# Loading order and first steps of a two-block fp32 kernel: token tiles in 2, 2, 2, 4, 6 columns on two queues, a first granule in two halves, a zero copy on ScalarE, three zero products on TensorE

## The reference

```python
h = rms_norm(x, ln_pre_g[layer])                        # x: 256 x 2048
proj = jnp.einsum('bsd,de->bse', h, w_in[layer])        # the first products of the program
rnn_x, rnn_gate, q, k, v, attn_gate, g_rnn, g_attn = split_columns(proj)
```

## Time and profile before

| | before |
|---|---|
| median of 3 runs | 2542.69 us (2540.52 to 2544.24) |
| time of the profiled execution | 2541.07 us |
| its span in the profile | 2539.3 us |
| TensorE busy | 2508.7 us, 99% |
| VectorE busy | 1946.3 us, 77% |
| ScalarE busy | 1273.2 us, 50% |
| first product of weights starts at | 10.16 us |

### The profile page before, as it was taken

One profiled execution on the slowest core, in us unless ns is written; L12 is line 12 of the kernel. 1 busy time (PEld: TensorE's weight loads), 2 busy tenths in 40 slices (PEclk: granted clock), 3 DMA queues, 4 the chain that ended last, 5 costly groups with the idle time before them and its releaser, 6 DMA issues.

```text
span 2539.3 us, 30959 instructions
## 1 busy us (share of the span) xinstructions
PE 2508.7 (99%) x11974; PEld 2047.7 (81%) x11974; DVE 1946.3 (77%) x2685; ACT 1273.2 (50%) x1754; POOL 98.8 (4%) x143
## 2 busy tenths in 40 slices
PE   8999999999999999999999999999999999999998
PEld 6778777888888888888888888778888888888887
DVE  6776776887776777566978768998985887998866
ACT  6544544545553444455456644436565454455654
POOL 0000000000000000000200000200000000200000
PEclk9999999999999999999999999999999999999999
DMA  9887798566556666676555568654446879544454
GB/s 351 307 308 261 252 317 279 196 215 216 194 182 239 234 241 242 234 258 230 182 164 165 171 244 290 236 166 150 157 145 245 292 257 348 198 147 153 149 190 174
DMA packets 350594, 570.15 MB, mean 225 GB/s; under 512 B 18224, under 2 KB 202800, under 8 KB 346608
## 3 DMA queue, kind: packets, MB, share of 16 engines
q1 hardware_dynamic: 343216, 532.84, 61.2%
q0 software_dynamic: 6512, 34.59, 3.8%
q10 hardware_dynamic: 720, 0.75, 0.1%
HBM read 559.69 MB, written 8.41 MB: 224 GB/s over the span
## 4 chain that ended last, share of the span: by engine, by line
PE 91%; DVE 3%; DMA 3%; ACT 1%; issue 1%; POOL 0%; SPq 0%; DVEq 0%; ACTq 0%
PE acc L587 27%; PE acc L589 27%; PE acc L588 27%; PE aux L1236 2%; PE aux L1261 1%; DVE w_lo L575 1%; DVE rows_u L2142 1%; PE aux L1018 1%; PE aux L1385 1%; DMA xr_s<-x_mid 1%; DMA xr_s<-c_mid 1%; PE aux L1246 1%; DMA rows_in<-in_w_mod 1%; PE aux L880 1%; ACT w_hi L567 0%
## 5 line engine op out<-in xcount | busy, mean ns | idle before, releaser
L575 DVE TENSOR_TENSOR w_lo<-raw,w_hi 128x1024 fp32r<-128x1024 f32 x808 | 990.6, 1229 | 446.5 <-ACT w_hi L567 444.5
L567 ACT ACTIVATE w_hi<-raw 128x1024 fp32r<-128x1024 f32 x808 | 847.1, 1059 | 870.2 <-PE acc L589 806.2
L587 PE MATMUL acc<-w_hi,h_hi 128*128 128x512 f32 x2240 | 893.1, 399 | 15.6 <-DVE w_lo L575 15.6
L589 PE MATMUL acc<-w_hi,h_lo 128*128 128x512 f32 x2240 | 875.4, 391 | 0.0
L588 PE MATMUL acc<-w_lo,h_hi 128*128 128x512 f32 x2240 | 874.3, 390 | 0.0
L587 PEld LDWEIGHTS acc<-w_hi,h_hi 128*128 128x128 f32 x2240 | 422.1, 188 | 120.9 <-issue 26.6
L589 PEld LDWEIGHTS acc<-w_hi,h_lo 128*128 128x128 f32 x2240 | 421.6, 188 | 90.1
L588 PEld LDWEIGHTS acc<-w_lo,h_hi 128*128 128x128 f32 x2240 | 422.5, 189 | 83.7
L587 PE MATMUL acc<-w_hi,u_hi 128*128 128x512 f32 x800 | 318.8, 398 | 1.5 <-DVE w_lo L575 1.4
L589 PE MATMUL acc<-w_hi,u_lo 128*128 128x512 f32 x800 | 312.1, 390 | 0.0
L588 PE MATMUL acc<-w_lo,u_hi 128*128 128x512 f32 x800 | 311.8, 390 | 0.0
(11 more groups left out here) (356 smaller groups left out, 2016.8 us busy)
## 6 DMA issues: line engine op xcount, KB each, us to landing
raw<-in_w_in SPq DMA_DIRECT2D x631, 512.0 KB, 4.7
raw<-in_w_mod SPq DMA_DIRECT2D x112, 512.0 KB, 6.2
raw<-in_w_out SPq DMA_DIRECT2D x96, 512.0 KB, 4.7
rows_in<-in_w_mod SPq DMA_DIRECT2D x80, 512.0 KB, 6.7
raw<-in_w_rnn_out SPq DMA_DIRECT2D x32, 512.0 KB, 4.6
raw<-in_w_o SPq DMA_DIRECT2D x32, 512.0 KB, 5.7
raw<-in_w_attn_out SPq DMA_DIRECT2D x16, 512.0 KB, 5.7
xr_s<-x_mid POOLq DMA_DIRECT2D x4, 1024.0 KB, 13.7
```

Source lines behind the costliest of these rows:

```text
L567: act.activation(w_hi[:, n % NSPLIT], raw[:, slot, (n % 2) * SK:(n % 2) * SK + SK], ACT.Copy).then_inc(hi_ready, 1)
L575: dve.tensor_tensor(w_lo[:, n % NSPLIT], raw[:, slot, (n % 2) * SK:(n % 2) * SK + SK], w_hi[:, n % NSPLIT].bitcast(F32), ALU.subtract).the ...
L587: pe.matmul(acc[pair][m][:, :], a_hi[:, k0 + k, tok], w_hi[:, s, k], start=b, stop=False)
L589: last = pe.matmul(acc[pair][m][:, :], a_lo[:, k0 + k, tok], w_hi[:, s, k], start=False, stop=e)
```

## The change

- **Turned tokens.** Five transfers of 2, 2, 2, 4 and 6 column tiles. The first is issued by ScalarE on its own queue, ahead of its constants; the others by SyncE, between the parts of pairs 0, 1 and 3.
- **First granule by k tile.** The two k tiles of granule 0 come in transfers of 256 KB with a semaphore each; ScalarE copies, VectorE subtracts and TensorE multiplies them one by one. The count of `lo_ready` is one higher from then on. Pair 1 comes in parts too, with granule 2 signalled by itself.
- **Zero copy.** ScalarE copies one column of zeros before its first wait on the tokens, which puts the table load there.
- **Zero products.** TensorE does three instead of one.
- **Constants.** `cols_b`, `ident` and `modbias` are issued by ScalarE after `hi` of granules 3, 4 and 5, and share one semaphore: who needs one of them waits for all three.
- **Straight tokens and tables.** `xr` is issued behind pair 5 and pair 6 instead of pair 4 and pair 5. Both transfers, `rope1` and `mask1` share one semaphore, `x_in`: who needs one of them waits for all four (64).

```diff
+TOKEN_ENDS = (0, 2, 4, 6, 10, 16)
+WARM = 3
...
-            if n == 0 and fresh:
-                act.wait_ge(first_raw, 16)
-            elif n % 2 == 0 or fresh and n == 1:
+            if n == 2 and fresh:
+                act.wait_ge(early_raw[2], 16)
+            elif n % 2 == 0 and (n or not fresh) or fresh and n in (1, 3):
...
+            if n == 0 and fresh:
+
+                for k in range(SK):
+                    act.wait_ge(early_raw[k], 16)
+                    act.activation(w_hi[:, 0, k], raw[:, slot, k], ACT.Copy).then_inc(hi_ready, 1)
+                return
...
+            if q + n == 0:
+
+                for k in range(SK):
+                    dve.wait_ge(hi_ready, k + 1)
+                    dve.tensor_tensor(w_lo[:, 0, k], raw[:, slot, k], w_hi[:, 0, k].bitcast(F32), ALU.subtract).then_inc(lo_ready, 1)
+                return
...
+                if q + n == 0:
+                    pe.wait_ge(lo_ready, k + 1)
...
-                sp.dma_start(xr[:, m], t["x"][0][m * P:(m + 1) * P, :]).then_inc((x_in, x_in1)[m], 16)
+                sp.dma_start(xr[:, m], t["x"][0][m * P:(m + 1) * P, :]).then_inc(x_in, 16)
...
-                if place in (NLOAD, NLOAD + 1):
-                    tokens(place - NLOAD)
+                if place in (NLOAD + 1, NLOAD + 2):
+                    tokens(place - NLOAD - 1)
                 if kind == "pair" and i == 5:
-                    sp.dma_start(rope1[:, :, :, :], t["rope_table"]).then_inc(table_in, 16)
-                    sp.dma_start(mask1[:, :, :], t["dilated_masks"]).then_inc(table_in, 16)
+                    sp.dma_start(rope1[:, :, :, :], t["rope_table"]).then_inc(x_in, 16)
+                    sp.dma_start(mask1[:, :, :], t["dilated_masks"]).then_inc(x_in, 16)
...
-            pe.matmul(X[3][:, :], modchunk[:, 0:P], modchunk[:, :], start=True, stop=True)
+            for _ in range(WARM):
+                pe.matmul(X[3][:, :], modchunk[:, 0:P], modchunk[:, :], start=True, stop=True)
...
+            act.dma_start(xT[:, 0:TOKEN_ENDS[1], :], t["x_columns"][:, 0:TOKEN_ENDS[1], :]).then_inc(xT_in[0], 16)
             act.dma_start(cols_a[:, :], t["columns"][:, 0:P]).then_inc(cols_a_in, 16)
...
+            act.wait_ge(mod_zero, 1)
+            act.activation(small[:, 41:42], modchunk[:, 0:1], ACT.Copy)
...
                 hi(act, Q1, b, b < NSPLIT)
+                if b == 3:
+                    act.dma_start(cols_b[:, 0:COLS_B], t["columns"][:, P:P + COLS_B]).then_inc(cols_b_in, 16)
+                elif b == 4:
+                    act.dma_start(ident[:, :], t["identity"]).then_inc(cols_b_in, 16)
+                elif b == 5:
+                    act.dma_start(modbias[:, :], t["columns"][:, P + COLS_B:P + COLS_B + 2 * LAYERS * KT]).then_inc(cols_b_in, 16)
...
-                        act.wait_ge((x_in, x_in1)[m], 16)
+                        act.wait_ge(x_in, 64)
                         act.activation(xr[:, m], xr[:, m], ACT.Square, accum_out=small[:, m:m + 1]).then_inc(ss_ready, 1)
...
-                dve.wait_ge(table_in, 32)
+                dve.wait_ge(x_in, 64)
```

More of the change, by code:

```diff
@@ L403, in build_program @@
         hi_ready, lo_ready, split_used = (sem(n) for n in ("hi_ready", "lo_ready", "split_used"))
-        const_in, x_in, xT_in = sem("const_in"), sem("x_in"), [sem(f"xT_in{i}") for i in range(4)]
-        cols_a_in, cols_b_in, first_raw = sem("cols_a_in"), sem("cols_b_in"), sem("first_raw")
+        x_in, xT_in = sem("x_in"), [sem(f"xT_in{i}") for i in range(5)]
+        cols_a_in, cols_b_in, early_raw = sem("cols_a_in"), sem("cols_b_in"), [sem(f"early_raw{i}") for i in range(3)]
         sp_ready, spn_ready, token_scale = sem("sp_ready"), sem("spn_ready"), sem("token_scale")
@@ L445, in build_program @@
         cv_sig, smod_r = sem("cv_sig"), sem("smod_r")
-        table_in, x_in1 = sem("table_in"), sem("x_in1")
         weighted, final_rstd, results = sem("weighted"), sem("final_rstd"), [sem(f"result{i}") for i in range(3)]
@@ L487, in load @@
                 if kind == "pair":
-                    sp.wait_ge(lo_ready, 2 * i + 2)
+                    sp.wait_ge(lo_ready, 2 * i + 3)
                 elif kind == "part":
@@ L572, in lo @@
             slot = slot_of(("pair", (q + n) // 2))
-            dve.wait_ge(hi_ready, q + (n + 1))
+            if q + n == 0:
[3 more added lines that the diff above has]
+                return
+            dve.wait_ge(hi_ready, q + (n + 2))
             dve.tensor_tensor(w_lo[:, n % NSPLIT], raw[:, slot, (n % 2) * SK:(n % 2) * SK + SK],
@@ L578, in products @@
         def products(pe, q, n, pair, k0, a_hi, a_lo, start, stop, tiles=range(NT)):
-            pe.wait_ge(lo_ready, q + (n + 1))
+            if q + n:
+                pe.wait_ge(lo_ready, q + (n + 2))
             s = n % NSPLIT
             for k in range(SK):
+                if q + n == 0:
+                    pe.wait_ge(lo_ready, k + 1)
                 for m in tiles:
@@ L621, in turned_tokens @@
             def turned_tokens(g):
-                k = slice(LK * g, LK * (g + 1))
+                k = slice(TOKEN_ENDS[g], TOKEN_ENDS[g + 1])
                 sp.dma_start(xT[:, k, :], t["x_columns"][:, k, :]).then_inc(xT_in[g], 16)
             def tokens(m):
-                sp.dma_start(xr[:, m], t["x"][0][m * P:(m + 1) * P, :]).then_inc((x_in, x_in1)[m], 16)
+                sp.dma_start(xr[:, m], t["x"][0][m * P:(m + 1) * P, :]).then_inc(x_in, 16)
             def gate_weights(it):
@@ L686, in _ @@
                 place = PLACE[item]
[L687 to L691, removed]
+                if place == 3:
+                    turned_tokens(4)
+                if place < 2:
+                    src = ktiles(w1, place, ds(0, CH))
+                    if place == 0:
+                        for k in range(SK):
+                            sp.dma_start(raw[:, 0, k, :], src[:, k, :]).then_inc(early_raw[k], 16)
+                    else:
+                        sp.dma_start(raw[:, 1, 0:SK, :], src[:, 0:SK, :]).then_inc(early_raw[2], 16)
+                    turned_tokens(1 + 2 * place)
                     for k in (2, 3):
-                        sp.dma_start(raw[:, 0, k, :], src[:, k, :]).then_inc(raw_ready[0], 16)
+                        sp.dma_start(raw[:, place, k, :], src[:, k, :]).then_inc(raw_ready[place], 16)
+                    if place == 0:
+                        turned_tokens(2)
                 elif kind == "pair":
@@ L949, in t_rnn @@
                 if first:
-                    pe.wait_ge(const_in, 16)
+                    pe.wait_ge(cols_b_in, 48)
                 else:
@@ L1103, in branch_granule @@
                 if n == 8:
-                    pe.wait_ge(table_in, 32)
+                    pe.wait_ge(x_in, 64)
                     pe.wait_ge(ev1_act, CH1 * IT1)
@@ L1458, in norm_sides @@
                     norm_high(s + 1, n - batches - 2, aff, dst)
+            act.dma_start(xT[:, 0:TOKEN_ENDS[1], :], t["x_columns"][:, 0:TOKEN_ENDS[1], :]).then_inc(xT_in[0], 16)
             act.dma_start(cols_a[:, :], t["columns"][:, 0:P]).then_inc(cols_a_in, 16)
-            act.dma_start(cols_b[:, 0:COLS_B], t["columns"][:, P:P + COLS_B]).then_inc(cols_b_in, 16)
-            act.dma_start(ident[:, :], t["identity"]).then_inc(const_in, 16)
-            act.dma_start(modbias[:, :], t["columns"][:, P + COLS_B:P + COLS_B + 2 * LAYERS * KT]).then_inc(cols_b_in, 16)
+            act.wait_ge(mod_zero, 1)
+            act.activation(small[:, 41:42], modchunk[:, 0:1], ACT.Copy)
             act.wait_ge(cols_a_in, 16)
             for b in range(8):
-                if b % 2 == 0:
-                    act.wait_ge(xT_in[b // 2], 16)
+                if 2 * b in TOKEN_ENDS:
+                    act.wait_ge(xT_in[TOKEN_ENDS.index(2 * b)], 16)
                 for k in (2 * b, 2 * b + 1):
@@ L1547, in iteration @@
                     if first and n == 8:
-                        act.wait_ge(cols_b_in, 32)
+                        act.wait_ge(cols_b_in, 48)
                         act.activation(scs[:, :], cols_b[:, CV:CV + 2 * KT], ACT.Sigmoid).then_inc(cv_sig, 1)
@@ L2200, in iteration @@
                     if first and n == 8:
-                        dve.wait_ge(cols_b_in, 32)
+                        dve.wait_ge(cols_b_in, 48)
                         softplus_start()
```

## The result

| | before | changed |
|---|---|---|
| median | 2542.69 us (9 runs, 2540.52 to 2549.40) | 2549.57 us (9 runs, 2546.19 to 2552.72) |
| ratio to before | | 1.0022, 95% interval 1.0013 to 1.0030 |
| profiled execution | 2541.07 us, span 2539.3 us | 2551.47 us, span 2549.7 us |
| TensorE busy | 2508.7 us, 99% | 2517.2 us, 99% |

The account below looks back on a forecast made before the run. TensorE is 99% busy, but ScalarE and VectorE lead from 33 to 95 us. Sums of squares +3.9, less 0.3 for the emptier queue, start not counted: +3.6 us, 2546.3 us from 2542.69, range 2540 to 2549.5.

Parts of the forecast that it names:

- The chain: From 33 us to 95 us ScalarE and VectorE lead, not TensorE; what hangs on them and is late stays late.
- wait before granule 11: TensorE, ahead from the start, waits 1.2 to 2.4 us for granule 11's w_lo, and its gain is gone.
- The term that decides: ScalarE's first sum of squares waits for the last straight tokens, landing at 37.3 instead of starting at 33.38: 3.9 us late.
- second queue: Issuing on ScalarE's queue adds no bandwidth; if it did, the last straight tokens would land 0.7 us earlier.
- The deduction: Loads of w_mod after the late sums land up to 0.9 us sooner in an emptier queue; 0.3 was taken off.
- The start: First product at 8.9 instead of 10.16 us; TensorE 1.2 to 2.4 us ahead by granule 1, not counted in the sum.
- All of it or nothing: Three zero products keep TensorE's clock high for the first products, saving 1.2 us wholly or not at all.
- Rival B: Clock falls in TensorE's new waits, and slow products after the tile at 59 us outlast the chain: +5.3, 2548.0; chance 0.22.
- Rival A: The straight tokens land in time and the start's gain stays: -1.2 to -2.4, say 2540.5; chance 0.15.
- C: The delay is worn off by slack in VectorE's row before 95 us: about 2542.5; chance 0.08.
- within 0.2%: Whole time within 0.2% (5 us) of before, on the slow side; chance 0.76.
- slower by over 0.2%: Whole time more than 0.2% above before, most of it from the clock falling in new waits; chance 0.2.

Follow-up runs that it names:

- x_early_apart: Changed kernel with straight tokens behind pair 4 and pair 5 again and each sum of squares waiting for its own half alone; ratio to before 0.9993.
- x_later_shared: Changed kernel with the second half of the straight tokens one pair further back, behind pair 7; ratio to before 1.0030.
- second profile: Changed kernel run and profiled once more, with nothing altered; ratio to before 1.0014, +3.6 us.
- before_late_shared: Kernel before with straight tokens behind pair 5 and pair 6 and one shared wait for both halves and both tables, old start kept; ratio to before 1.0012.
- x_late_apart: Changed kernel with its order of loads, but each sum of squares waiting for its own half alone; ratio to before 1.0008.
- x_early_shared: Changed kernel with straight tokens behind pair 4 and pair 5 again, shared wait for both halves and both tables kept; ratio to before 1.0007.
- x_early_apart_warm1: The kernel x_early_apart with one zero product instead of three; ratio to before 0.9997.

## Why the prediction was right, and where it was short

**The chain.** That the time from 33 to 95 us is led by ScalarE and VectorE and not by TensorE is the step on which all rested, and it is shown: the delay at granule 12 follows the start of the sums of squares to a tenth in six profiles of five kernels (4.48 and 4.5, 4.10 and 4.1, 7.73 and 7.7, 4.17 and 4.2, 1.36 and 1.4, and 1.78 and 1.8 by the second sum), and at granule 28 it is there within 0.5, save the 1.3 of one transfer in one profile. From x_early_apart to x_later_shared the ratios rise with it from 0.9993 to 1.0030. And TensorE's own lead does not count: its wait before granule 11 is 3.57, 1.21 and 6.49 us in three profiles with the new start, and the delay is that of the sums of squares each time.

**The term that decides.** The landing was put at 37.3, where the last half of pair 6 had landed, and the delay at 3.9. Measured were 37.86 and 37.48, delays of 4.5 and 4.1. The mechanism, the same bytes in another order in a full queue, held: the DMA engines have no gap there (share 0.97 or more in every stretch of 2 us from 8 to 42 us), and one more pair, 1 MB, ahead of the load in `x_later_shared` moves it by 3.3 to 3.6 us more. The term was 0.2 to 0.6 too small. No bandwidth of a second queue shows: had it added bandwidth, the landing would have been 0.7 us sooner, at 36.6, and it was later than 37.3.

**The deduction.** I took 0.3 off for an emptier queue. In the second profile, 4.1 shrank to 3.7 on the way to granule 28, in before_late_shared 4.2 to 4.0. But in x_late_apart and x_later_shared nothing came off (1.8 and 1.8, 7.7 and 7.8), and in the first profile and x_early_shared the delay grew, by 1.3 and 0.5. So the deduction is not borne out as a term; where something came off, it was 0.2 to 0.4.

**The start.** First product foretold at 8.9, measured at 8.38: the first transfers landed sooner (cols_a let h_hi go at 5.74; I had taken 6.3, from 5.8 to 6.8). In the second profile it let h_hi go at 6.09, and the first product stands at 8.74. The zero products took 5.49 and 5.30 us instead of 6.2. "All of it or nothing" for the clock came out both ways: up from the first product on in one profile, down from 9.8 to 13 us in the other. So the wait before granule 11 was 3.57 us in the one and 1.21 in the other, where I had 1.2 to 2.4, and nothing came of the difference, as forecast.

**The rivals.** Rival B has the number nearest to the first set of runs (2548.0 against 2548.3), but not by its mechanism. It wanted a wait of 2.4 to 3 us for the tile at 59 us and slow products behind it. In the first profile TensorE has no such wait; in the second it waits 1.01 us, until 59.02; the clock is 1.00 from 50 to 64 us in both. The clock did fall at granule 11, at 42 us, in the first profile, and was back at 48; those slow products were hidden by the chain, as the prediction said. Rival A (tokens in time) and C (worn off) did not come about. What A would have been worth is tested by x_early_apart: at granule 28 it is 0.4 us late, and of A's 1.2 to 2.4 us nothing shows there; its time, 1.8 us faster, does not tell A's price from none.

**What is short.** The prediction was +3.6 us; the two sets of runs say +5.6 (3.3 to 7.6) and +3.6 (1.3 to 5.8). I gave 0.76 to "within 0.2%", where the second set lies (0.14%), and 0.2 to "slower by over 0.2%", where the first lies (0.22%, with 0.13% as its lower end). The mechanism of the sum held. Its sizes fell short in two places: the term of the sums of squares, by 0.2 to 0.6 us, and all that lies beyond 95 us, for which the sum has no term. In the first profile the delay is 5.8 us at granule 28 and 10.4 at the end; in the second it is 3.7 and 4.5, after a stretch at 5.8 to 6.0. The largest single step between is at 781 us, where TensorE waits 2.5 us for VectorE in every profile. In that of before, the clock stayed up, and the products behind the wait stand 0.23 to 0.24 us apart:

```profile
775.78 1.17 PE L918 MATMUL aux<-ident,s_sb 128*128 128x128 f32 x9 [2.47 <-DVE og L2058]
...
777.02 0.40 PE L588 MATMUL acc<-w_lo,u_hi 128*128 128x512 f32 x1
777.26 0.39 PE L589 MATMUL acc<-w_hi,u_lo 128*128 128x512 f32 x1
```

In the first profile of the change it fell (the last row is a window, with the granted clock behind the count), the products stand 0.43 us apart, and the granules behind them are another 1.6 us later:

```profile
781.48 1.68 PE L941 MATMUL aux<-ident,s_sb 128*128 128x128 f32 x9 [2.48 <-DVE og L2088]
...
783.81 0.63 PE L605 MATMUL acc<-w_hi,u_lo 128*128 128x512 f32 x1
784.24 0.63 PE L603 MATMUL acc<-w_hi,u_hi 128*128 128x512 f32 x1
```

```profile
780.00:784.00 4.00, 2.52 (x12) 0.75 0.00 0
```

The clock fell there in 7 of 12 profiles: in both of the changed kernel and in five with its start, but not in before_late_shared nor in three others with that start. Whether the change makes it likelier, by moving everything ahead of it, can't be told from so few; it is not settled whether anything is left of the difference once such steps are evened out.

**Where the start's gain goes.** Even with the straight tokens in time it is not seen in the profiles by granule 28, nor clearly in the times: the ratios of the four kernels with tokens in time are 0.9993 to 0.9998, each with 1 inside its interval, and a gain of up to some 4 us is not excluded. In the kernels with the new start TensorE begins 1.4 to 1.8 us earlier and granule 2 is split 1.6 to 2.5 us earlier, but from 10 to 48 us the DMA queue is full (share 0.97 to 1.19 in every stretch of 2 us, before and with the change), and granule 6 is split no earlier than before (0 to 0.8 us later). With the tokens in time the chain is within 0.7 us of where it was at granule 28, and not ahead at the last tile of w_mod. That the queue holds it is what ScalarE's wait on pair 5 shows at granule 10; further on (granules 12 to 28) it is argued from TensorE's and VectorE's waits on w_mod, and was not taken away by itself.

## What to carry to other kernels

A semaphore shared by several loads turns a wait for the first into a wait for the last, and a load moved back in a full queue lands later by all the bytes that now stand ahead of it: here 4.1 to 4.5 us, more than twice the 1.4 to 1.8 us by which the first product came earlier. Before the start of a kernel is tuned, follow the chain of waits beyond it: here a lead of the busiest engine was worth nothing that the runs can show, since other engines and a full queue lead a few granules on. When semaphores are short, let loads share one that are issued next to each other and needed at the same time.

## What was not expected of the hardware

- The three zero products took between 4.3 and 5.5 us in eight profiles with the same start, and what was left as a wait before the first product went with the clock there: after waits of 1.5 to 1.8 us (four profiles) it stayed up, after 2.1 to 2.9 us (four, the second one of the change among them: 0.94 from 8 to 10 us, 0.50 from 10 to 12) it fell. Which of the two, the wait or the moment at which the zero products ended, decides is not shown, as they come together.
- A wait of TensorE of 2.5 us at the same place left the clock up in five profiles and was followed by a fall in seven (0.75 over the 4 us in the first profile of the change); the length of the wait alone does not decide. The longer waits, 3.57 us up to 42 us and 6.49 us in x_later_shared up to 45 us, were both followed by windows at 0.50.
- Windows of the profile early in an execution can show 1.00 although the products in them stand 0.43 us apart (x_early_apart_warm1, 8 to 14 us). There the spacing has to be read, not the clock.
